# Down panels by output half, and the last couple's output half by half

## The reference, cut to what matters

```python
def expert_block(args):
    xb, e = args
    return (jax.nn.silu(xb @ w_g[e]) * (xb @ w_u[e])) @ w_d[e]
...
out = jnp.zeros((T, D), h.dtype).at[slot_tok].add(ys * slot_w[:, None])
...
x = x + hierarchical_moe(rmsnorm(x, ffn_norm[l]), ...)
return rmsnorm(x, final_norm)
```

## Time and profile before

| | us |
|---|---|
| median of 3 runs | 792.1 |
| lowest and highest | 790.5, 795.67 |
| the profiled execution, whole | 794.2 |
| its span, first to last instruction | 792.4 |
| PE busy | 691.7 (87%) |
| DVE, ACT, POOL busy | 354.9, 325.6, 386.7 |
| DMA over the span | 229 GB/s |

### The profile page before, as it was taken

The page is one execution under the profiler, slowest core; times in us unless marked ns, Lnnn a source line. Parts: engine busy times, 40 slices in busy tenths (PEclk is TensorE's granted clock), DMA queues, the critical chain, the costliest instruction groups (busy, mean ns, idle before and its releaser), DMA issues.

```text
span 792.4 us, 13896 instructions
## 1 busy us (share of the span) xinstructions
PE 691.7 (87%) x5658; PEld 578.0 (73%) x5658; DVE 354.9 (45%) x657; ACT 325.6 (41%) x589; POOL 386.7 (49%) x284
## 2 busy tenths in 40 slices
PE   3799999999999989699988999989799997777764
PEld 3789989889989988699777899989654544333421
DVE  1788964489997131610692554561520111001002
ACT  5434566875464334445434766432312121111112
POOL 2656865588879978098597656695000000000000
PEclk9978999999999999799988999999999999999998
DMA  8613543433344445045343433489979999999992
GB/s 331 248 54 107 167 148 112 158 109 124 142 161 158 162 160 172 41 160 191 129 160 107 160 108 117 150 356 419 380 274 423 421 421 420 422 421 423 421 422 117
DMA packets 26131, 181.73 MB, mean 229 GB/s; under 512 B 3025, under 2 KB 3281, under 8 KB 4561
## 3 DMA queue, kind: packets, MB, share of 16 engines
q1 hardware_dynamic: 26064, 180.81, 59.9%
HBM read 179.75 MB, written 1.05 MB: 228 GB/s over the span
## 4 chain that ended last, share of the span: by engine, by line
PE 60%; DMA 15%; DVE 13%; ACT 5%; issue 4%; SPq 1%; POOL 0%; ACTq 0%; DVEq 0%
PE D L447 39%; PE L L832 4%; DMA ring<-w_expert_dram 4%; DMA hT<-w_expert_dram 4%; DMA wu<-w_expert_dram 4%; DMA big<-w_expert_dram 3%; PE L L812 3%; DVE big_r L1328 2%; PE QB L862 2%; PE UB L488 1%; DVE big_r L1333 1%; PE L L575 1%; DVE big L1469 1%; SPq L386 1%; DVE big L1309 1%
## 5 line engine op out<-in xcount | busy, mean ns | idle before, releaser
L1292 POOL TENSOR_TENSOR ring_r<-ring,ring_r 128x512 fp32r<-128x512 f32 x280 | 386.5, 1410 | 161.0 <-ACT ring_r L950 160.4
L447 PE MATMUL D<-scr_r,ring_r 128*128 128x256 f32 x1248 | 239.7, 289 | 1.7 <-ACT big L1179 0.9
L950 ACT ACTIVATE ring_r<-ring 128x1024 fp32r<-128x1024 f32 x140 | 147.3, 1057 | 151.4 <-PE D L447 133.1
L447 PEld LDWEIGHTS D<-scr_r,ring_r 128*128 128x128 f32 x1248 | 199.1, 193 | 4.6 <-issue 2.1
L447 PE MATMUL D<-hT_r,ring_r 128*128 128x256 f32 x624 | 177.3, 284 | 0.0
L447 PE MATMUL D<-big_r,ring_r 128*128 128x256 f32 x1158 | 146.8, 288 | 9.8 <-DVE big L1600 5.2
L447 PEld LDWEIGHTS D<-big_r,ring_r 128*128 128x128 f32 x1158 | 143.8, 196 | 11.4 <-DVE big L1600 5.6
L447 PEld LDWEIGHTS D<-hT_r,ring_r 128*128 128x128 f32 x624 | 120.5, 193 | 1.2 <-issue 1.0
L1309 DVE SCALAR_TENSOR_TENSOR th<-th,L 64x256 f32<-64x256 f32 x32 | 13.4, 418 | 179.1 <-ACT th L1223 178.5
L1223 ACT ACTIVATE th<-L 64x256 f32<-64x256 f32 x16 | 6.0, 378 | 85.7 <-PE L L832 85.7
L812 PEld LDWEIGHTS L<-cst,big 128*128 128x128 f32 x256 | 29.8, 191 | 12.2 <-issue 10.7
(11 more groups left out here) (302 smaller groups left out, 934.5 us busy)
## 6 DMA issues: line engine op xcount, KB each, us to landing
ring<-w_dense_dram SPq DMA_DIRECT2D x70, 1024.0 KB, 4.9
big<-w_expert_dram SPq DMA_DIRECT2D x40, 1024.0 KB, 25.8
ring<-w_expert_dram SPq DMA_DIRECT2D x30, 1024.0 KB, 26.2
wu<-w_expert_dram SPq DMA_DIRECT2D x6, 1024.0 KB, 25.1
attn<-w_expert_dram SPq DMA_DIRECT2D x5, 1024.0 KB, 21.3
scr<-w_expert_dram SPq DMA_DIRECT2D x5, 1024.0 KB, 27.0
hT<-w_expert_dram SPq DMA_DIRECT2D x5, 1024.0 KB, 27.3
xT<-w_expert_dram SPq DMA_DIRECT2D x5, 1024.0 KB, 27.6
```

The source lines that it names most:

```text
L447: last = mm(out_, r32(w[i][ws]), r32(x[j][xs_]), start=start and m == 0, stop=stop and m == 2)
L950: A_(r32(hi_unit(j)), dense_unit(j), ACT.Copy).then_inc(hi_ready, 1)
L1292: last = g.tensor_tensor(r32(w), w, r32(h).bitcast(F32), ALU.subtract)
```

## The change

The two down panels of a couple no longer hold one expert each, but one output half of both experts. In fifteen couples `down` reads the same numbers from other places. For the last couple:

- PE: `last_down(0)` takes the panel with half 0 and writes each chunk `k` and expert `e` to a row group of its own, with no adding in PSUM; `last_combine(0)` adds all 128 rows into `ACC[tt][0]` for both tiles, so the two chunks are summed there. Then `last_down(1)` into the bank `X`, and `last_combine(1)`.
- ACT: right after the last tanh a root of two numbers that nobody reads, which brings the root's table. After the last couple's copy the squares of half 0, then the copy of `X` to the other `ye`, then the squares of half 1, one root for both tiles, and the scaling of half 0 out of `y_out`, which ACT also stores, with its own DMA issues.
- VectorE: half 0 times the gain as soon as it is squared; then one add and one reciprocal for both tiles, and the scaling of half 1, which SP stores.

```diff
+        half_scaled = sem("first_half_scaled")
...
-            for n in range(2 * NT):
-                sp_.wait_ge(out_scaled, n + 1)
-                sp_.dma_start(out[:, n * 512:(n + 1) * 512], y_out[:, n // 2, (n % 2) * 512:(n % 2 + 1) * 512]
-                              ).then_inc(stored, 16)
+            for tt in range(NT):
+                sp_.wait_ge(out_scaled, tt + 1)
+                sp_.dma_start(out[:, (2 * tt + 1) * 512:(2 * tt + 2) * 512], y_out[:, tt, 512:1024]).then_inc(stored, 16)
...
             def down(p, b):
-                w = [expert_panel(pe, 6 * p + 4 + e).rearrange("p (k h f) -> p k h f", k=2, h=2) for e in range(2)]
+                w = [expert_panel(pe, 6 * p + 4 + h).rearrange("p (e k f) -> p e k f", e=2, k=2) for h in range(2)]
...
-                            last = mm(DN[at_:at_ + WIN, :], actT[:, b, k, e * WIN:(e + 1) * WIN], w[e][:, k, h, :],
+                            last = mm(DN[at_:at_ + WIN, :], actT[:, b, k, e * WIN:(e + 1) * WIN], w[h][:, e, k, :],
...
+            def last_down(h):
+
+                w = expert_panel(pe, PANELS - 2 + h).rearrange("p (e k f) -> p e k f", e=2, k=2)
+                for k in range(2):
+                    for e in range(2):
+                        at_ = (2 * k + e) * WIN
+                        last = mm((DN, X)[h][at_:at_ + WIN, :], actT[:, (PAIRS - 1) % 2, k, e * WIN:(e + 1) * WIN],
+                                  w[:, e, k, :], start=True, stop=True)
+                last.then_inc(y_mm, 1)
+
+            def last_combine(h):
+
+                pe.wait_ge(ye_ready, PAIRS + h)
+                for tt in range(NT):
+                    mm(ACC[tt][h][:, :], swT[:, (PAIRS - 1) % 2, tt * P:(tt + 1) * P], ye[:, 1 - h, :],
+                       start=False, stop=True, skip_group_check=True).then_inc(x2_ready, 1)
...
-                    down(p, p % 2).then_inc(y_mm, 1)
                     if p + 1 < PAIRS:
+                        down(p, p % 2).then_inc(y_mm, 1)
                         sw_transposes(p + 1, release=2)
-                pe.wait_ge(ye_ready, PAIRS)
-                pe.wait_ge(swt_ready, PAIRS)
-                for tt in range(NT):
-                    add_experts((PAIRS - 1) % 2, tt, True).then_inc(x2_ready, 1)
+                last_down(0)
+                last_combine(0)
+                last_down(1)
+                last_combine(1)
...
+            def out_squares(h):
+                for tt in range(NT):
+                    act.wait_ge(x2_ready, 2 * h + tt + 1)
+                    scratch = y_out[:, tt, 512:1024] if h else th[:, tt, :]
+                    A_(scratch, ACC[tt][h][:, :], ACT.Square, accum_out=stat[:, tt, 0, h:h + 1]).then_inc(x2_sq, 1)
+
             def layer_out():
...
+                act.wait_ge(x2_ms, 1)
+                A_(stat[:, :, 2, 0], stat[:, :, 1, 0], ACT.Sqrt, bias=sp[:, 9, 0:1], scale=1.0 / D).then_inc(x2_root, 1)
+                act.wait_ge(x2_inv, 1)
                 for tt in range(NT):
...
+                    A_(y_out[:, tt, 0:512], y_out[:, tt, 0:512], ACT.Copy, scale=stat[:, tt, 1, 1:2]).then_inc(half_scaled, 1)
+                    act.wait_ge(half_scaled, tt + 1)
+                    act.dma_start(out[:, 2 * tt * 512:(2 * tt + 1) * 512], y_out[:, tt, 0:512]).then_inc(stored, 16)
...
                     gate_tanh(p % 2).then_inc(gate_t, 1)
+                    if p + 1 == PAIRS:
+                        A_(stat[:, :, 2, 0], sp[:, 9, 0:2], ACT.Sqrt)
...
+                out_squares(0)
+                act.wait_ge(y_mm, PAIRS + 1)
+                act.wait_ge(comb, PAIRS - 1)
+                A_(ye[:, 0, :], X[:, :], ACT.Copy).then_inc(ye_ready, 1)
+                out_squares(1)
                 layer_out()
...
             def layer_out():
+                dve.wait_ge(s_in["last_gain"], 16)
                 for tt in range(NT):
...
                     dve.wait_ge(x2_sq, tt + 1)
...
+                    last = v.tensor_tensor(y_out[:, tt, 0:512], ACC[tt][0][:, :], last_gain[:, 0:512], ALU.mult)
+                dve.wait_ge(x2_sq, 2 * NT)
+                v.tensor_tensor(stat[:, :, 1, 0], stat[:, :, 0, 0], stat[:, :, 0, 1], ALU.add).then_inc(x2_ms, 1)
+                dve.wait_ge(x2_root, 1)
+                v.reciprocal(stat[:, :, 1, 1], stat[:, :, 2, 0]).then_inc(x2_inv, 1)
+                dve.wait_ge(x2_inv, 1)
+                for tt in range(NT):
+                    stt(y_out[:, tt, 512:1024], ACC[tt][1][:, :], stat[:, tt, 1, 1:2],
+                        last_gain[:, 512:1024]).then_inc(out_scaled, 1)
...
-    dn = down.reshape(NE, 2, P, D).transpose(0, 2, 1, 3).reshape(NE, P, 2 * UNIT)
+    dn = down.reshape(PAIRS, 2, 2, P, 2, 512).transpose(0, 4, 3, 1, 2, 5).reshape(PAIRS, 2, P, 2 * UNIT)
```

More of the change, by code:

```diff
@@ L861, in down, with add_experts @@
                             at_ = (2 * h + e) * WIN
-                            last = mm(DN[at_:at_ + WIN, :], actT[:, b, k, e * WIN:(e + 1) * WIN], w[e][:, k, h, :],
+                            last = mm(DN[at_:at_ + WIN, :], actT[:, b, k, e * WIN:(e + 1) * WIN], w[h][:, e, k, :],
                                       start=(k == 0), stop=(k == 1))
                 return last
-            def add_experts(b, tt, stop):
+            def last_down(h):
[11 more added lines that the diff above has]
+                       start=False, stop=True, skip_group_check=True).then_inc(x2_ready, 1)
+            def add_experts(b, tt):
                 for h in range(2):
@@ L869, in add_experts @@
                     last = mm(ACC[tt][h][:, :], swT[rows, b, tt * P:(tt + 1) * P], ye[rows, b, :],
-                              start=False, stop=stop, skip_group_check=True)
+                              start=False, stop=False, skip_group_check=True)
                 return last
@@ L875, in combine @@
                 pe.wait_ge(swt_ready, p + 1)
-                add_experts(p % 2, 0, False)
-                add_experts(p % 2, 1, False).then_inc(comb, 1)
+                add_experts(p % 2, 0)
+                add_experts(p % 2, 1).then_inc(comb, 1)
             pe.wait_ge(htok_ready, 4)
@@ L927, in _ @@
                         pe.wait_ge(ye_ready, w)
-                        add_experts(0, 0, False)
-                        add_experts(0, 1, False).then_inc(comb, 1)
+                        add_experts(0, 0)
+                        add_experts(0, 1).then_inc(comb, 1)
                     pe.wait_ge(comb, (p + 1) * WINDOWS)
                     nc.tensor.transpose(M[:, 0:P], ident, ident).then_inc(panel_used, 6)
-                for tt in range(NT):
-                    nc.tensor.transpose(M[:, tt * P:(tt + 1) * P], ident, ident).then_inc(x2_ready, 1)
+                for n in range(2 * NT):
+                    nc.tensor.transpose(M[:, 0:P], ident, ident).then_inc(x2_ready, 1)
         @block.scalar
@@ L1752, in layer_out @@
             def layer_out():
+                dve.wait_ge(s_in["last_gain"], 16)
                 for tt in range(NT):
-                    ms, inv = stat[:, tt, 1, 0:1], stat[:, tt, 1, 1:2]
                     dve.wait_ge(x2_sq, tt + 1)
[L1756 to L1764, removed]
+                    last = v.tensor_tensor(y_out[:, tt, 0:512], ACC[tt][0][:, :], last_gain[:, 0:512], ALU.mult)
[7 more added lines that the diff above has]
+                        last_gain[:, 512:1024]).then_inc(out_scaled, 1)
             uncrowded = dve.value_load(rt[0:1, 544:545].bitcast(I32), min_val=0, max_val=1)
@@ L1873, in pack @@
     gu = np.stack([gate, up], 1).reshape(NE, 2, 2, 4, P, FF).transpose(0, 2, 4, 1, 3, 5).reshape(NE, 2, P, 2 * UNIT)
-    dn = down.reshape(NE, 2, P, D).transpose(0, 2, 1, 3).reshape(NE, P, 2 * UNIT)
+    dn = down.reshape(PAIRS, 2, 2, P, 2, 512).transpose(0, 4, 3, 1, 2, 5).reshape(PAIRS, 2, P, 2 * UNIT)
     order = []
     for e in range(0, NE, 2):
-        order += [gu[e, 0], gu[e + 1, 0], gu[e, 1], gu[e + 1, 1], dn[e], dn[e + 1]]
+        order += [gu[e, 0], gu[e + 1, 0], gu[e, 1], gu[e + 1, 1], dn[e // 2, 0], dn[e // 2, 1]]
     expert = np.stack(order)
```

8 lines of the change are left out of this document (removed).

## The result

The kernel after takes 795.28 us (median of 22 runs, 793.13 to 796.43), the kernel before 792.28 (22 runs, 790.5 to 795.67). The ratio is 1.0031, with a 95% interval from 1.0021 to 1.004: slower by 1.7 to 3.2 us. I had forecast 793.2 against 792.1, 1.1 us slower. The sign, the range and the class (within 1%) were right, the size was not: by this timing the loss is two to three times what I summed. A second timing on another occasion gave 1.0012 (0.9996 to 1.0027).

The account below looks back on a forecast made before the run. Full DMA engines bound the kernel, leaving only the 13.8 us tail to change. The chain gains 0.2 us up to scaling, but bunched stores end the span at 793.5 against 792.4, so 793.2 against the median, range 790.3 to 796.0.

Parts of the forecast that it names:

- Where the chain starts: Start of `last_down(0)` on PE, after ACT's copy of the transposes: 778.45 instead of 778.74, 0.3 us gained.
- The hidden load: ACT's table load between last tanh and copy: hidden by 0.3 us, freeing the first root's 1.28 us on the path.
- the other fifteen couples cost nothing: Their `down` waits for both panels as before, with the same instructions on other columns: costed at nothing.
- Steps 1 to 8: Tail from `last_down(0)` to the first store's issue at 788.32: 0.2 us gained up to the second tile's half's scaling.
- step 6: `last_combine(1)` on PE: first tile to ACT at 785.15, second at 786.11, add on VectorE at 786.82.
- The stores: Output stores at the end: all four ready together, 1 MB in 2.76 us at 377 GB/s, last landing 793.1.
- The span ends 0.4 after that: End of the program: span ends 0.4 us after the last store lands at 793.1, so 793.5 against 792.4.
- Setting the span's difference against the median: Whole-kernel time: the span's difference of 1.1 us, set against the median of 792.1, gives 793.2.
- the gain after all: Rival, tail: load and second root go, stores not limited by their rate; time 791.5; chance 1 in 12.
- The table load is longer than its row: Rival, ACT before the copy: 1.38 us more drain delays the copy, all 1.0 later, 794.2; chance 1 in 14.
- The half clock: Rival, PE in the tail: `last_down(1)` and `last_combine(1)` take twice their rounds, 2.6 us more, 795.8; chance 1 in 25.

Follow-up runs that it names:

- the second trace: The kernel after, unchanged, profiled and timed again: tail 15.7 us, median 794.19 us, ratio to the kernel before 1.0012.
- the early table alone: Kernel before with only the small root right after the last tanh, run twice: tails 12.7 and 12.8 us, ratios 0.9996 and 0.9983.
- the best: Kernel after reworked: both downs first, VectorE's second copy, combine tile by tile, a root per tile, SP's paired stores; tails 12.6 and 12.9 us, ratios 0.9989 and 0.9988.
- the semaphore: Kernel before with one more semaphore allocated and not used: tail 14.0 us, median 792.87 us, ratio 1.0003.

## Why the prediction was right in sign and short in size

Point by point, as times after the start of ACT's copy (summed as I had it, then measured in the first trace of after):

| step | summed | measured |
|---|---|---|
| `last_down(0)` starts | 0.33 | 0.33 |
| ACT's copy | 1.45 | 1.46 |
| `last_combine(0)` | 2.10 | 2.11 |
| `last_down(1)` | 4.02 | 4.02 |
| ACT's second copy | 5.14 | 5.16 |
| `last_combine(1)` | 5.79 | 5.81 |
| add on VectorE | 8.70 | 8.55 |
| scaling starts | 9.41 | 9.28 |
| first and last store issued | 10.17, 11.3 | 10.03, 11.24 |
| bytes from, to | 11.0, 13.8 | 10.9, 13.9 (10.9, 14.3 in the second trace) |
| SP past the stores | 15.0 | 14.4 (14.7 in the second trace) |
| ACT at the end of the block | not in the sum | 15.4 |
| end of the span | 15.4 | 15.7 |

- **Where the chain starts:** right after the copy (0.33), but the 0.3 us gained there is a gain only over a trace in which PE waits for the last panel. Where the last gate-and-up half runs at half clock, as in both traces of after, the kernel before starts at 0.33 too, and the term is nothing.
- **The hidden load:** right. So is the claim that the other fifteen couples cost nothing: the panels by half alone leave the tail at 14.0.
- **Steps 1 to 8:** right within 0.15 us. The 0.15 is in step 6: I took 0.96 between the squares of two tiles, from the starts of the matmuls; PE does start them 0.96 apart, but the first tile's matmuls take 1.12 and the second's 0.10 less, so the results are 0.86 apart, as the chain shows (782.06, 0.87).
- **The stores:** the rate was near (370 GB/s over 2.5 us, at 0.97 of the engines, but 3.0 us from first byte to last, 3.4 in the second trace, for the 2.76 summed). The 1.2 us from the last byte to the landing were a misreading. I had let the second pair's bytes end at 790.8 before the change; the trace of before shows them still moving after 791:

```profile
791.00:791.50 0.50, 0.00 (x0) 0.00 (x0) 0.00 (x0) 0.00 (x0) 0.00 (x0) 0.50 0.16 49
```

From the last byte to SP's passing it is 0.4 to 0.5 us in the first two traces of each kernel. The two errors together put SP's passing 0.3 to 0.6 too late: 14.4 and 14.7 measured, 15.0 summed.
- **"The span ends 0.4 after that": this step failed.** It took SP for the last engine at the barrier, because it was before. With a store as its last instruction, ACT became the last. Its DRAIN came 0.8 and 0.6 us after SP's (15.4 against 14.6 and 14.9), and with one store less on ACT the same issues end 0.65 us sooner. I had asked what waits behind the new instructions on ACT's queue and answered that nobody does; the end of the program did.
- **Setting the span's difference against the median: this failed too.** I took the 1.8 us outside the span as the same for both. It is 2.19 after, 1.81 before, in every run of either (2.12 to 2.33 and 1.74 to 1.92).

The account from the tails: 1.4 to 1.7 us of tail (15.7 against 14.3 and 14.0; 1.7 is the comparison of like with like) and 0.37 outside the span make 1.8 to 2.1 us, 1.0023 to 1.0026 of the time, inside both measured intervals. That the sum of 1.1 came as near as it did is in part luck: the stores sized too long hid part of ACT's exit. The first timing's 3.0 us between the medians is not fully accounted for. The level of the last gate-and-up half may be in it, since from the start of that half to the end the kernel before takes 18.5 us at the full clock and 19.7 at half, but the timed runs do not tell their level.

Of the rivals, the gain after all did not come, though its premise was sound: the load was worth 1.35 to 1.46 us when taken alone, and the rest of the change took back more. "The table load is longer than its row" is refuted by the ten traces of the seven kernels that have it early. The half clock fell on the gate-and-up half ahead of the tail and not on its matmuls: the rounds of `last_combine(1)` start 0.43 to 0.53 apart. That level came in traces of both kernels.

## What to carry to other kernels

Splitting the last piece of work so that a first half can run earlier buys a second trip through every hand-over, and it costs most when the second half is queued behind the first half's consumers: issuing both producers first, then both consumers, took back 1.9 us here. Even so no form of the split ended earlier than the early table alone (12.6 and 12.9 for the best, 12.7 and 12.8 for the table). Look at what each engine does last: an engine that is given a last small job starts to leave later by it, and may then leave the program last, with an exit that takes longer than the job. And of a change made of several parts, time each on the base alone; here the early table alone gave 1.35 to 1.46 us of tail, and the rest spent more than that.

## What the runs showed of the hardware that I had not expected

- From its jump out of the last branch to its DRAIN an engine takes up to 3.9 us, and part of that can lie under its last work. ACT takes 3.6 to 3.8 in the four traces in which it stores and 2.6 to 3.3 in the other ten. PE takes 3.3 to 3.9 in all 14, with no store moving. VectorE takes 3.7 in the first trace of before (787.77 to 791.46, its last scaling ends at 789.16), and 0.57 in the kernel after (784.43 to 785.00). What makes the short case is open.
- SP's issue of a 256 KB store takes 0.33 to 0.35 us throughout the four traces of the kernel before, of the new panels and of the semaphore, where the stores of a pair are 0.66 apart. The distance does not decide it: with the same 0.66 the second store took 0.71 and 0.55 with the early table and 1.09 in the second trace of after, and one took 1.51 when SP stored all four.
- Four stores of 256 KB together move at 370 GB/s, no faster than two did before (377), although two engines issued them and one before.
- The time outside the first and last instruction is a property of the program: 1.77 to 1.85 in five kernels, 2.18 to 2.24 in five, with no run between 1.95 and 2.12.
